# The opening of a one-core encoder block: the odd tiles of x move to ScalarE's DMA queue

## The reference

```
h = RMSNorm(x)              # x * rsqrt(mean(x*x) + eps) * norm_w
[qA,kA,vA,zA, qB,kB,vB,zB, aB,bB, gate] = h @ W_in
yA = DiffAttn(qA,kA,vA) * silu(zA)
yB = RMSNorm(GatedDeltaNet(conv(qB,kB,vB), aB, bB)) * silu(zB)
m  = sigmoid(gate_A) * (yA @ W_upA) + sigmoid(gate_B) * (yB @ W_upB)
x  = x + m @ W_out
```

## Time and profile before

| | |
|---|---|
| median of 3 runs | 944.63 us |
| profiled execution | 944.84 us |
| its span, first to last instruction | 942.8 us |
| busy: PE, PE weight loads, VectorE, ScalarE, GpSimd | 928.7, 767.1, 604.1, 368.0, 292.6 us |
| three passes of the projections (L1334, L1336, L1338 with h) | 312.2, 314.8, 313.7 us |
| DMA, mean over the span | 62 GB/s |
| DMA in the first of 40 slices (23.6 us) | 230 GB/s |

### The profile page before, as it was taken

How to read it: one execution, slowest core, us unless ns; L and a number is a source line. 1 busy time by engine, 2 the same in 40 slices (tenths; PEclk the granted TensorE clock), 3 DMA queues, 4 the chain that set the end, 5 groups by cost and what they waited for, 6 DMA issues and landing times.

```text
span 942.8 us, 15129 instructions
## 1 busy us (share of the span) xinstructions
PE 928.7 (99%) x5283; PEld 767.1 (81%) x5283; DVE 604.1 (64%) x1406; ACT 368.0 (39%) x782; POOL 292.6 (31%) x225
## 2 busy tenths in 40 slices
PE   7999999999999999999999999999999999999998
PEld 6788888888788888888887888888888878888887
DVE  6777677647565667656726465566466567555995
ACT  5422333343333333432334554465455562122341
POOL 4222233453222222222125133232132123233652
PEclk9999999999999999999999999999999999999999
DMA  6112112212211121221101111111101113334503
GB/s 230 34 46 54 44 44 46 54 48 57 67 57 35 56 67 36 67 54 38 57 23 35 34 24 34 34 24 34 34 25 34 48 32 112 112 112 167 222 1 133
DMA packets 73000, 58.12 MB, mean 62 GB/s; under 512 B 4114, under 2 KB 62700, under 8 KB 72940
## 3 DMA queue, kind: packets, MB, share of 16 engines
q1 hardware_dynamic: 70700, 55.23, 19.9%
q10 hardware_dynamic: 2240, 2.12, 0.9%
HBM read 48.93 MB, written 8.40 MB: 61 GB/s over the span
## 4 chain that ended last, share of the span: by engine, by line
PE 94%; DVE 2%; ACT 1%; POOL 1%; issue 1%; DMA 1%; SPq 0%; ACTq 0%; POOLq 0%
PE PS L1336 22%; PE PS L1334 22%; PE PS L1338 22%; PE PS L1651 3%; PE PS L1676 3%; PE PS L1794 3%; PE PS L1796 3%; PE PS L1795 3%; PE PS L1669 2%; PE PS L1480 1%; PE PS L1508 1%; PE PS L1479 1%; PE PS L1501 1%; PE PS L1407 1%; PE PS L1522 1%; PE PS L1528 1%
## 5 line engine op out<-in xcount | busy, mean ns | idle before, releaser
L1336 PE MATMUL PS<-h_lo,w_hi 128*128 128x512 f32 x784 | 314.8, 402 | 0.0
L1334 PE MATMUL PS<-h_hi,w_hi 128*128 128x512 f32 x784 | 312.2, 398 | 2.6 <-POOL w_lo L714 1.6
L1338 PE MATMUL PS<-h_hi,w_lo 128*128 128x512 f32 x784 | 313.7, 400 | 0.0
L714 POOL TENSOR_TENSOR w_lo<-w_raw,w_hi 128x512 fp32r<-128x512 f32 x100 | 147.5, 1475 | 441.5 <-ACT w_hi L867 440.5
L1334 PEld LDWEIGHTS PS<-h_hi,w_hi 128*128 128x128 f32 x784 | 147.5, 188 | 33.9 <-issue 2.4
L1336 PEld LDWEIGHTS PS<-h_lo,w_hi 128*128 128x128 f32 x784 | 147.5, 188 | 28.1 <-issue 0.7
L1338 PEld LDWEIGHTS PS<-h_hi,w_lo 128*128 128x128 f32 x784 | 147.7, 188 | 27.2 <-issue 0.8
L867 ACT ACTIVATE w_hi<-w_raw 128x512 fp32r<-128x512 f32 x100 | 62.7, 627 | 47.6 <-PE PS L1338 43.7
L2201 DVE TENSOR_REDUCE mx<-PS 128x1 f32<-128x1024 f32 (+7 forms) x64 | 48.4, 756 | 49.7 <-PE PS L1656 49.7
L1917 DVE SCALAR_TENSOR_TENSOR acc<-pre,cw,acc 128x1024 f32<-128x1024 f32 x36 | 56.2, 1562 | 1.3
L1135 ACT ACTIVATE prob<-PS,nm,r_qk 128x1024 f32<-128x1024 f32 (+7 forms) x64 | 52.6, 829 | 5.5 <-DVE nm L2205 5.3
(11 more groups left out here) (288 smaller groups left out, 1561.4 us busy)
## 6 DMA issues: line engine op xcount, KB each, us to landing
w_raw<-in_w_in SPq DMA_DIRECT2D x98, 256.0 KB, 2.8
x_in<-in_x SPq DMA_DIRECT2D x8, 512.0 KB, 7.8
zv<-gate_dram SPq DMA_DIRECT2D x8, 512.0 KB, 3.4
out_sb<-in_x SPq DMA_DIRECT2D x4, 1024.0 KB, 12.7
out<-out_sb SPq DMA_DIRECT2D x16, 256.0 KB, 2.2
gate_dram<-gate_st SPq DMA_DIRECT2D x7, 512.0 KB, 2.9
grow<-g_dram ACTq DMA_DIRECT2D x8, 256.0 KB, 3.2
w_raw<-in_w_up_gdn SPq DMA_DIRECT2D x8, 256.0 KB, 2.9
```

What stands on the lines that cost most here:

```text
L714: pool.tensor_tensor(lo[:, b, :], w_raw[:, b, :], hi[:, b, :].bitcast(F32), ALU.subtract)\
L1334: pe.matmul(dst, w, hi, start=first, stop=False)
L1336: pe.matmul(dst, w, lo, start=False, stop=False)
L1338: mm = pe.matmul(dst, lo_w, hi, start=False, stop=last)
```

## The change

Sync issues the even tiles and the slabs, ScalarE the odd tiles, ahead of its load of `norm_w`. Nothing else is changed; the semaphores and those who wait for them are the same.

```
             def load_x(t):
                 sp.dma_start(x_in[:, t, :], x_rows[t * P:(t + 1) * P, :]).then_inc(x_loaded[t].sem, 16)
 
+            X_BY_SP = (0, 2, 4, 6)
+
...
-            for t in range(NT // 2):
+            for t in X_BY_SP[:2]:
                 load_x(t)
             load_tile(0, COL_QB)
-            for t in range(NT // 2, NT):
+            for t in X_BY_SP[2:]:
                 load_x(t)
...
         @block.scalar
         def _(act):
+            for t in (1, 3, 5, 7):
+                act.dma_start(x_in[:, t, :], x_rows[t * P:(t + 1) * P, :]).then_inc(x_loaded[t].sem, 16)
             act.dma_start(vec[:, 48:56], norm_w[0].rearrange("(k p) -> p k", p=P), allow_slow_non_contiguous=True).then_inc(norm_loaded.sem, 16)
             act.wait_ge(consts_ready.sem, 2)
```

## The result

| | before | after |
|---|---|---|
| median of 12 runs (lowest to highest) | 944.68 us (944.38 to 945.41) | 947.02 us (946.71 to 947.49) |
| span of the profiled execution | 942.8 us | 945.5 us |
| mean granted TensorE clock | 1.000 | 0.998 |
| h_lo 6 of the first projection starts | 21.34 | 23.44 |

The changed kernel is slower by 2.3 us: ratio 1.0024, 95% interval 1.0016 to 1.0032. Nearly all of it is there by the seventh step of the first projection. The opening first, on ScalarE, beside the earlier trace rows. Columns of a timeline: start, length, engine, line, operation, then the idle time before it and what ended it.

The account below looks back on a forecast made before the run. TensorE, busy 99%, bounds the kernel, so only the start of its gapless run, set by h_lo 6, counts. norm_w's late landing gives +2.0 us, the rest lies under it: 946.6 us, range 944.1 to 948.3.

Parts of the forecast that it names:

- (a): Opening, DMA issue: four issues move from Sync to ScalarE, which is still early for x1's square; costs nothing.
- (b): Opening, first tiles: x0 and x1 both land at 5.6; scaling 3 starts +0.1 us, between -0.8 and +0.6.
- (c): Opening, ScalarE: norm_w lands last, at 16.1, so h_hi 0 starts 2.8 us late and h_lo 6 +2.0 (+1.3 to +2.7).
- the spare: Between h_hi 6, done by 20.5, and h_lo 6, started at 21.34: 0.8 us of lateness absorbed.
- The lower bound of the landing, 15.4: Earliest landing of norm_w, from a tile at 393 GB/s taking 1.33: 4.7 + 10.6 + 0.7 - 0.6.
- (d): Opening, VectorE: x4 lands at 14.6, its square delays h_lo 0, +1.0 us alone; hidden under norm_w's lateness.
- (e): Opening, weight slabs: they land at 11.9 and 12.9, w_hi ends before norm_w lands, GpSimd's pair ends at 16.6; costs nothing.
- R1: Rival, DMA queues: several small packets go per turn, norm_w lands at 14.2; 944.9 us (944.3 to 945.2), chance 0.22.
- R2: Rival, opening: x0 as early as alone, nothing late behind, scaling 3 starts 0.8 us earlier; 943.8 us, chance 0.06.
- R3: Rival, TensorE clock: half pace after a 3.3 us idle wait adds +1.3 us on norm_w's lateness; 947.9 us, chance 0.10.
- The sum of +2.0: Whole kernel: norm_w's lateness gives +2.0 us, every other step lies under it; 946.6 us.

Follow-up runs that it names:

- e4: Changed kernel with GpSimd's second w_lo moved behind the power of tile 4; median +1.85 us against the kernel before, ratio 1.0009 to 1.0026.
- e7: Kernel before, one queue, with norm_w issued by Sync behind x7; median +3.0 us against the kernel before, ratio 1.0019 to 1.0040.
- e9: Changed kernel with norm_w not awaited and the second w_lo behind the power of tile 4; median +1.1 us against the kernel before.
- e8: Changed kernel with norm_w still loaded but not awaited, h scaled by ones; median +2.3 us against the kernel before.
- e2: Changed kernel with x4 issued ahead of the slabs on Sync's queue; +1.87 us against the kernel before, ratio 1.0010 to 1.0027.
- e11: Kernel before with norm_w issued by Sync between x3 and the slabs, second w_lo behind the power of tile 4; -0.10 us against the kernel before.
- e3: Changed kernel with norm_w first on ScalarE's queue and x4 before the slabs on Sync's; +2.24 us against the kernel before.
- e10: Kernel before with GpSimd's second w_lo behind the power of tile 4; median -0.2 us against the kernel before, ratio 0.9989 to 1.0007.
- e5: Changed kernel with 14 more identity products on TensorE ahead of tile 3's last transpose; median +2.0 us against the kernel before.
- e6: Kernel before, one queue, with norm_w issued by Sync between x3 and the slabs; -0.03 us against the kernel before.
- e12: e11 with 6 more identity products on TensorE ahead of tile 3's last transpose; -0.38 us against the kernel before, ratio 0.9987 to 1.0005.
- e1: Changed kernel with norm_w issued first on ScalarE's queue, before x1, x3, x5, x7; +1.67 us against the kernel before.

## Why the prediction was right, and where it was not

*(a) issue time* was right: x1's square started at its landing, 5.79.

*(b) the first tiles*: both within 0.2 us of each other, at 5.95 and 5.77 where 5.6 was taken. Scaling 3 started at 12.61, +0.5 instead of +0.1, inside the bounds. It decided nothing.

*(c) norm_w at the back* was right in its mechanism and a little large in its size. The packets go in turn, norm_w landed at 15.7 (16.1 forecast) and h_hi 0 started 2.5 late (2.8). h_hi 6, at 22.37, was 2.54 late, and less the spare that is 1.8 at h_lo 6 (2.0 forecast). e4, where x4's square has its normal length and norm_w came at 16.0, tests the rest of the step: h_hi 6 2.84 late, h_lo 6 2.08 late. That is 2.8 less 0.8, as forecast. e7 shows nearly the same cost, 1.89, without a second queue. The lower bound of the landing, 15.4, takes off 0.6 us where the sentence before it allows 0.8; nothing turned on it.

*(d) x4 late* holds the step that failed: "It lies under (c)". x4's landing was right to 0.1 us (14.7, 14.6 forecast), and its price alone as well (1.09 in e9, +1.0 forecast). But the step costed the square of x4 at its old 1.23 us. (e) put GpSimd's w_lo at 13.1 to 16.6, and (d) put the square at 14.6; the two times stood in the text, and that they meet wasn't weighed. The square took 2.27, h_lo 0 came at 17.12 instead of 16.8, and (d) was no longer under (c) but over it, as e8 shows (2.13 with norm_w not awaited). Where norm_w bounds, h_lo 6 starts 0.75 us after h_hi 6 (e2, e4, e7); in the kernel after it is 1.07. So the 2.10 came from x4 and its slow square, and norm_w alone would have given about 1.8, an estimate from 22.37 + 0.75. That the forecast of +2.0 fits so well is luck: (c) was 0.2 too large and (d) 1.1 too small, and the larger of the two came out where (c) had been put.

*(e) the slabs* was right: they landed at 12.2 and 13.35 (11.9 and 12.9 forecast), and ScalarE's w_hi waited for them, but nothing waited for w_hi. GpSimd's pair took 2.49 instead of 3.51, since here the square of x4 was the later of the two.

*R1* is refuted by the packet counts, *R2* by x0 at 5.95 and x4 at 14.7. *R3* came true in its cause and not in its price. TensorE did go on at 1.2 GHz after its 3.51 us pause, with its steps at twice their distance, which the prediction had named as a sign that it is wrong. It had priced the lower clock at +1.3; measured was 0.15 to 0.2 (PE +2.26 to +2.29 against h_lo 6 +2.10), because the seventh step waits for h_lo 6 at 23.4 whatever the six before it take, as long as they are through by then. Where h_lo 6 comes sooner, the same clock costs about 0.4 (e9: 1.52 against 1.09; e11: -0.01 against -0.38).

The sum of +2.0 stands beside a measured +2.34. Of the difference, 0.1 is h_lo 6 and 0.2 the clock; the rest is inside what the medians can tell.

## What to carry to other kernels

A second DMA queue brought no bytes here, where the DMA engines were already full: with one queue and norm_w at its end (e7) everything was in by 15.85, with two (after) by 16.06. It changed the order in which loads land. Write down both queues packet by packet, and look at whatever gets later: here one small load with 4-byte packets at the end of a queue cost about 2 us, and so did one tile that came 1.9 us late, though about half of that only because its square met an instruction of another engine. When an instruction is moved in time, ask what runs on the neighbour engine at its new time before giving it its old duration. And when two causes of one size lie side by side, taking away either shows nothing; take away both.

## What the runs showed of the hardware that was not expected

- VectorE's square of a 128x1024 tile and GpSimd's w_lo hold each other up. The square takes 1.22 to 1.23 us where no w_lo runs when it starts (before, e2, e3, e4, e7, e9, e10) and 1.87 to 2.31 where one does (after, e5, e6, e8, e11, e12). In e1, with 1.35, the w_lo that was running had only 0.27 us left. Where the square came first, GpSimd paid: 2.21 instead of 1.27 for one w_lo (e10), 3.51 instead of 2.49 for two. The Trainium skill (SBUF — State Buffer, section Who interferes with whom) names the place, for a VectorE instruction with two inputs in SBUF, as this square has in the code (the tile twice): a port pair that the two engines share and that one instruction holds to its end. No run here shows the port; the trace agrees that the one which started second is the one that grows.
- A load of 1024 packets of 4 bytes at the head of a queue delays what stands behind it on that queue: x1 came at 8.3 in e1 and 9.4 in e3, 5.8 in the kernel after.
- The granted clock fell to half during the pause ahead of the first projection step or within 1.2 us of its end where TensorE had paused for 2.28 us (e6, e11), 2.29 (e1), 2.56 (e9), 2.79 (e2), 3.51 (after, e8) and 4.42 (e7). In e4 the first steps went at full pace after 3.10 us; there it had fallen earlier, among the transposes, from 9.55 to 12.97, after a pause of only 1.87. A pause of 2.86 us ahead of the first transpose in e2 was followed by no such fall. So the length of the pause alone doesn't decide; what does was not tried.
